# Where the first expert's weights, the prompt rows and the result tiles are moved, in a one-core mixture-of-experts step

## What is computed

```python
h2 = rms_norm(x, p['norm2_g']) * (1.0 + scale2[:, None]) + shift2[:, None]
x = x + gate2[:, None] * expert_choice_moe(h2, p['w_router'], p['w_exp_gate'], p['w_exp_up'], p['w_exp_down'])
...
    aff = jax.nn.softmax(jnp.einsum('bld,de->ble', h, w_router).astype(jnp.float32), axis=-1)
    gate, idx = lax.top_k(jnp.swapaxes(aff, 1, 2), cap)
    xs = jax.vmap(lambda hb, ib: hb[ib])(h, idx)
    hid = jax.nn.silu(jnp.einsum('becd,edf->becf', xs, w_gate)) * jnp.einsum('becd,edf->becf', xs, w_up)
    out = jnp.einsum('becf,efd->becd', hid, w_down) * gate[..., None].astype(h.dtype)
```

## Time and profile before

| what | value |
|---|---|
| median of 3 runs | 1992.8 us (1992.07 to 1993.43) |
| the profiled execution, its own time | 1993.96 us |
| its span, first to last instruction | 1992.1 us |
| mean granted TensorE clock | 0.976 |
| TensorE busy | 1906.3 us, 96% |
| VectorE busy | 1207.8 us, 61% |
| bytes read and written in DRAM | 633.46 MB and 15.38 MB |

### The profile page before, as it was taken

How to read it: one execution, slowest core, us unless ns; L and a number is a source line. 1 busy time by engine, 2 the same in 40 slices (tenths; PEclk the granted TensorE clock), 3 DMA queues, 4 the chain that set the end, 5 groups by cost and what they waited for, 6 DMA issues and landing times.

```text
span 1992.1 us, 64268 instructions
## 1 busy us (share of the span) xinstructions
PE 1906.3 (96%) x28594; PEld 1352.5 (68%) x28594; DVE 1207.8 (61%) x1966; ACT 395.3 (20%) x909; POOL 299.7 (15%) x316
## 2 busy tenths in 40 slices
PE   8999999999987999999999999999999999999996
PEld 5888899999873677777555555655556565555553
DVE  3532431232645777777677777767677676776764
ACT  4332333122320111111111111112111111111113
POOL 3032019000311010110101001010010101001002
PEclk8999999999988999999999999999999999999998
DMA  9254542322268999999999999999999999999996
GB/s 338 85 163 143 175 128 65 105 64 85 106 246 334 415 408 420 408 411 417 408 419 409 410 418 408 419 408 417 412 411 417 408 419 410 409 420 409 418 410 265
DMA packets 149503, 649.54 MB, mean 326 GB/s; under 512 B 9980, under 2 KB 54904, under 8 KB 133064
## 3 DMA queue, kind: packets, MB, share of 16 engines
q1 hardware_dynamic: 134576, 617.71, 77.0%
q0 software_dynamic: 14688, 30.98, 5.4%
q10 hardware_dynamic: 184, 0.06, 0.0%
HBM read 633.46 MB, written 15.38 MB: 326 GB/s over the span
## 4 chain that ended last, share of the span: by engine, by line
PE 43%; DMA 17%; SPq 4%; DVE 3%; issue 2%; POOL 1%; ACT 0%; DVEq 0%; POOLq 0%
PE bank L2327 17%; DMA ring<-in_w_exp_gate_dram 16%; PE bank L2355 13%; PE bank L2344 7%; PE bank L2337 5%; SPq L565 2%; SPq L572 2%; PE bank L2252 1%; DVE hid_t L1737 1%; DMA y_tile<-acc_scratch 1%; DVE sums L1672 1%; DVE hid L1741 0%; DMA x_g<-h_scratch,idx_all 0%; DVE hid_t L1744 0%; DVE hid L1734 0%
## 5 line engine op out<-in xcount | busy, mean ns | idle before, releaser
L1672 DVE TENSOR_TENSOR sums<-ring 128x704 f32<-128x704 f32 x744 | 610.4, 888 | 200.4 <-PE bank L2344 107.8
L2327 PE MATMUL bank<-ring,hid_t 128*32 128x256 f32 x8184 | 477.7, 390 | 38.7 <-DVE hid_t L1744 38.0
L2355 PE MATMUL bank<-ring,xs_t 128*32 128x352 f32 x5952 | 446.0, 459 | 0.0
L2327 PEld LDWEIGHTS bank<-ring,hid_t 128*32 128x32 f32 x8184 | 277.4, 113 | 211.9 <-DVE hid_t L1744 42.2
L2355 PEld LDWEIGHTS bank<-ring,xs_t 128*32 128x32 f32 x5952 | 198.9, 110 | 232.3 <-issue 182.3
L2344 PE MATMUL bank<-sums,xu_a 128*32 128x176 f32 x5952 | 245.1, 313 | 0.0
L2344 PEld LDWEIGHTS bank<-sums,xu_a 128*32 128x32 f32 x5952 | 194.2, 110 | 28.1
L775 POOL TENSOR_TENSOR small<-kpow 128x2 f32<-128x2 f32 x31 | 13.6, 438 | 1118.0 <-DVE out_rows L1803 882.2
L1143 ACT ACTIVATE v_both<-bank 128x176 f32<-128x176 f32 x31 | 9.8, 318 | 855.4 <-PE bank L2344 855.4
L1926 PE MATMUL bank<-act_hi,wt_hi 128*128 128x320 f32 x448 | 138.8, 310 | 0.8 <-DVE rtmp L1485 0.8
L1235 DVE TENSOR_TENSOR wt_lo<-raw_t,wt_hi 128x2048 fp32r<-128x2048 f32 x25 | 57.5, 2301 | 134.4 <-ACT wt_hi L864 134.4
(11 more groups left out here) (363 smaller groups left out, 2266.5 us busy)
## 6 DMA issues: line engine op xcount, KB each, us to landing
ring<-in_w_exp_gate_dram SPq DMA_DIRECT2D x128, 1408.0 KB, 26.1
ring<-in_w_exp_up_dram SPq DMA_DIRECT2D x128, 1408.0 KB, 27.8
ring<-in_w_exp_down_dram SPq DMA_DIRECT2D x96, 1536.0 KB, 24.9
ring<-in_w_exp_down_dram SPq DMA_DIRECT2D x32, 1024.0 KB, 27.3
raw_t<-in_w_ada_dram SPq DMA_DIRECT2D x16, 1024.0 KB, 5.2
raw_t<-in_w_in_dram SPq DMA_DIRECT2D x14, 1024.0 KB, 5.1
a_raw<-in_w_ada_dram SPq DMA_DIRECT2D x8, 1024.0 KB, 16.4
raw_t<-in_w_branch_gate_dram SPq DMA_DIRECT2D x8, 1024.0 KB, 5.4
```

The costliest lines, as they stand in the source:

```text
L1672: nc.vector.tensor_tensor(sums[:, (N_SUM * i + j) % SUM_SLOTS], w[:, k, :, n, :], w[:, kk, :, nn, :], ALU.add if sign > 0 else ALU.subtrac ...
L2327: ins = mm(bank[5 + x // 2][c * Q:(c + 1) * Q, x % 2 * DC:(x % 2 + 1) * DC], hid_t[:, f, x * Q:(x + 1) * Q], w[:, j, c * DC:(c + 1) * DC], ...
L2355: ins = mm(bank[UP_BANK[x]][c * Q:(c + 1) * Q, 0:FC], xs_t[:, x, k * Q:(k + 1) * Q], w[:, kk, c * FC:(c + 1) * FC], start=k == 0, stop=k = ...
```

## The change

- `FIRST` becomes 6. The first 8 pieces are g0, g1, u0 to u3 in slots 0 to 5, issued by SyncE, and g2, g3 in two new buffers (`extra`), issued by GpSimd once all x tiles have been written to DRAM. The buffers lie where `x2` was and `sums` will be. TensorE takes the sample groups in the order g0, g1, g2, g3, u0 to u3, and VectorE's first `sums` wait until both extra pieces are used. The rest of the stream goes into the ring from slot 6 on.
- The prompt group moves only its 16 tokens: four indirect DMAs of 16 rows in place of one of 128, in the gather and in the accumulating scatter.
- At the end the rows of the last expert are gathered first. The result tiles are loaded after the last weight piece has landed, the prompt's first. TensorE does the last piece of all three groups (prompt first) and then the three `row_sums`. ScalarE and VectorE start with the rows and take the tiles after them. The prompt rows are written after the prompt tile's store, the sample rows after the four sample stores.

The core of the diff (the helpers `y_root`, `row_square`, `row_root`, `row_sum`, `row_scale` and `y_scale` hold the instructions that stood in the loops at L1203 to L1216 and L1854 to L1875, one tile or group each):

```diff
-FIRST = 8
+FIRST = 6
+EARLY_PIECES = (("g", 0), ("g", 1), ("u", 0), ("u", 1), ("u", 2), ("u", 3), ("g", 2), ("g", 3))
+Y_ORDER = (4, 0, 1, 2, 3)
+ROW_ORDER = (2, 0, 1)
+NI = 6
...
+        extra = [at(f"extra{i}", A + 36864 + 12288 * i, [P, PIECE]) for i in range(2)]
         own_low = at("own_low", A + 59392, [P, 2, FN])
-        xu_a, xu_b = at("xu_a", 12288 + 8192, [P, KT // 2, 16, Q // 2]), at("xu_b", 98304 + 11264, [P, KT // 2, 4, Q // 2])
+        xu_a, xu_b = at("xu_a", 98304 + 8192, [P, KT // 2, 16, Q // 2]), at("xu_b", 122880 + 11264, [P, KT // 2, 4, Q // 2])
...
             for t in range(FIRST):
-                gate_up(t, t, t // 4, t % 4, 0, 0, 0)
+                gate_up(t, t, int(EARLY_PIECES[t][0] == "u"), EARLY_PIECES[t][1], 0, 0, 0)
...
-                down(STEPS * RING - 4 + i, FIRST + i, i, NE - 1, 1)
-
...
-                sp.wait_ge(s_y, lt + 1)
+                down((STEPS - 1) * RING + FIRST + i, FIRST + i, i, NE - 1, 1)
+
+            for j, lt in enumerate(Y_ORDER):
+                sp.wait_ge(s_y, j + 1)
                 dst = y_sample[0, lt * P:(lt + 1) * P, :] if lt < NS else y_prompt[0]
-                sp.dma_start(dst, y_tile[:, lt, :]).then_inc(s_out, 16)
-            sp.wait_ge(s_out, 16 * NT)
...
+            def prompt_slots(c):
+
+                return slice(c * Q, c * Q + C_P)
+
+            def gather_prompt(idx, source):
+
+                for c in range(4):
+                    pool.indirect_dma_start(x_g[prompt_slots(c), 2, :], None, source,
+                                            bass.IndirectOffsetOnAxis(idx[0:C_P, 2 + c:3 + c], 0)).then_inc(e_gath, 16)
...
-                    pool.indirect_dma_start(x_g[:, 2, :], None, h2_rows[0:4 * SPARE_END],
-                                            bass.IndirectOffsetOnAxis(idx_all[:, 0, 2:3], 0)).then_inc(e_gath, 16)
+                    gather_prompt(idx_all[:, 0, :], h2_rows[0:4 * SPARE_END])
...
             pool.wait_ge(s_acc, 16 * NT)
+            for t in range(FIRST, 8):
+                dst, landed = early_piece(t)
+                i = EARLY_PIECES[t][1]
+                pool.dma_start(dst[:, 0:2 * FH].rearrange("p (k f) -> p k f", f=FH),
+                               w_exp_gate[0, 0].rearrange("(p k) f -> p k f", k=KT)[:, 2 * i:2 * i + 2, FH:2 * FH])\
+                    .then_inc(landed, 16)
...
 
             def scatter():
-                for x in range(NX):
+                for x in range(2):
                     pool.indirect_dma_start(acc_rows, bass.IndirectOffsetOnAxis(idx_scatter[:, x:x + 1], 0), out_rows[:, x, :],
                                             None, compute_op=ALU.add).then_inc(s_acc, 16)
+                for c in range(4):
+                    pool.indirect_dma_start(acc_rows, bass.IndirectOffsetOnAxis(idx_scatter[0:C_P, 2 + c:3 + c], 0),
+                                            out_rows[prompt_slots(c), 2, :], None, compute_op=ALU.add).then_inc(s_acc, 16)
 
             pool.wait_ge(e_idx, 1)
...
-            for lt in range(NT):
-                pool.dma_start(y_tile[:, lt, :], acc_dram[scratch_rows(lt), :]).then_inc(s_fin[lt], 16)
+            pool.wait_ge(s_acc, 16 * NT + 16 * NI * (NE - 1))
...
             for x in range(NX):
                 pool.indirect_dma_start(x_g[:, x, :], None, acc_rows, bass.IndirectOffsetOnAxis(idx_all[:, NE - 1, x:x + 1], 0))\
                     .then_inc(e_gath, 16)
-            pool.wait_ge(s_out, 16 * NT)
-            for x in range(NX):
-                pool.wait_ge(s_rfin, x + 1)
+            pool.wait_ge(e_landed[FIRST + 3], 16 * STEPS)
+            for lt in Y_ORDER:
+                pool.dma_start(y_tile[:, lt, :], acc_dram[scratch_rows(lt), :]).then_inc(s_fin[lt], 16)
+            for j, x in enumerate(ROW_ORDER):
+                if j == 0:
+                    pool.wait_ge(s_outp, 16)
+                else:
+                    pool.wait_ge(s_out, 16 * NS)
...
-            act.wait_ge(e_used, RING + 3)
+            act.wait_ge(e_used, RING + 1)
             act.wait_ge(e_xt, 2)
             unit_copies(None, xs_t)
-            act.wait_ge(e_used, RING + 4)
+            act.wait_ge(e_extra, 2)
             for x in range(NX):
...
                   .then_inc(act_step, 1)
-                act.wait_ge(act_step, NT + lt + 1)
+                act.wait_ge(act_step, NT + j + 1)
                 nc.scalar.activation(small[:, 16 + lt:17 + lt], small[:, lt:lt + 1], ACT.Sqrt, bias=small[:, 46:47],
                                      scale=1.0 / D).then_inc(s_sqrt, 1)
-            for x in range(NX):
-                act.wait_ge(s_row, x + 1)
-                nc.scalar.activation(y_sq[:, x * DC:(x + 1) * DC], out_rows[:, x, :], ACT.Square,
+
+            def row_square(j):
+
+                x = ROW_ORDER[j]
+                act.wait_ge(s_row, j + 1)
+                nc.scalar.activation(hid[:, x, 0:DC], out_rows[:, x, :], ACT.Square,
                                      accum_out=small[:, 5 + x:6 + x]).then_inc(s_rsq, 1)
-                act.wait_ge(s_rsum, x + 1)
+
+            def row_root(j):
+
+                x = ROW_ORDER[j]
+                act.wait_ge(s_rsum, j + 1)
                 nc.scalar.activation(small[:, 8 + x:9 + x], bank[UP_BANK[x]][:, 0:1], ACT.Sqrt, bias=small[:, 46:47],
                                      scale=1.0 / D).then_inc(s_rroot, 1)
+
+            row_square(0)
+            row_square(1)
+            row_root(0)
+            y_root(0)
+            row_square(2)
+            row_root(1)
+            y_root(1)
+            row_root(2)
+            for j in range(2, NT):
+                y_root(j)
 
...
+            nc.vector.memset(x_g[:, 2, :], 0.0)
...
+                for c in range(1, 4) if group else ():
+                    nc.vector.tensor_scalar(idx_all[:, :, 2 + c], src[:, 0, :], 4.0, float(c), ALU.mult, ALU.add)
...
-            dve.wait_ge(e_used, RING + 3)
+            dve.wait_ge(e_used, RING + 1)
             nc.vector.memset(unit(V5)[:, :, Q // 2:], 0.0)
             nc.vector.memset(unit(V6)[:, :, 0:Q // 2], 0.0)
             unit_sums(xs_t, 1)
+            dve.wait_ge(e_extra, 2)
...
+            def y_scale(j):
+
+                lt = Y_ORDER[j]
+                dve.wait_ge(s_sqrt, 2 * NT + 1 + j + 1)
                 tick(nc.vector.reciprocal(small[:, 24 + lt:25 + lt], small[:, 16 + lt:17 + lt]))
                 nc.vector.scalar_tensor_tensor(out=y_tile[:, lt, :], in0=y_tile[:, lt, :], scalar=small[:, 24 + lt:25 + lt],
                                                in1=fg_b[:], op0=ALU.mult, op1=ALU.mult).then_inc(s_y, 1)
...
+            def row_sum(j):
+
+                x = ROW_ORDER[j]
+                dve.wait_ge(s_last, j + 1)
+                nc.vector.scalar_tensor_tensor(out=hid[:, x, 0:DC], in0=bank[x][:, 0:DC], scalar=gate_cur[:, x:x + 1],
+                                               in1=g2_q[:, x // 2, :], op0=ALU.mult, op1=ALU.mult).then_inc(e_out, 1)
+                dve.wait_ge(e_rows, NX * (NE - 1) + x + 1)
+                dve.wait_ge(e_out, done + NX + j + 1)
+                nc.vector.tensor_tensor(out_rows[:, x, :], out_rows[:, x, :], hid[:, x, 0:DC], ALU.add).then_inc(s_row, 1)
+
+            def row_scale(j):
+
+                x = ROW_ORDER[j]
+                dve.wait_ge(s_rroot, j + 1)
+                tick(nc.vector.reciprocal(small[:, 11 + x:12 + x], small[:, 8 + x:9 + x]))
+                nc.vector.scalar_tensor_tensor(out=out_rows[:, x, :], in0=out_rows[:, x, :], scalar=small[:, 11 + x:12 + x],
+                                               in1=fg_q[:], op0=ALU.mult, op1=ALU.mult).then_inc(s_rfin, 1)
+
+            dve.wait_ge(s_fg, 16 * 5)
+            dve.wait_ge(e_gath, 16 * NI * (NE - 1) + 80 + 16 * NX)
             for x in range(NX):
                 dve.wait_ge(e_out, done + x + 1)
...
+            for j in range(NX):
+                row_sum(j)
+            row_scale(0)
+            for j in range(NT):
+                y_scale(j)
+            row_scale(1)
+            row_scale(2)
...
+            def gate_up(t, tiles):
+
+                kind, i = EARLY_PIECES[t]
+                w = early_piece(t)[0][:, 0:2 * FH].rearrange("p (k f) -> p k f", f=FH)
...
-            for t in range(FIRST):
-                gate_up(t // 4, t % 4, t, (0, 1)).then_inc(e_used, 1)
+            for t in (0, 1, 6, 7, 2, 3, 4, 5):
+                gate_up(t, (0, 1)).then_inc(e_used if t < FIRST else e_extra, 1)
...
+            pe.wait_ge(e_landed[FIRST + 3], 16 * STEPS)
+            for x in ROW_ORDER:
+                down_last(x, 3).then_inc(s_last, 1)
+            for j in range(NX):
+                row_sums(j)
```

74 lines of the change are left out of this document (28 added, 46 removed).

## The result

The changed kernel took **2000.2 us** (median of 6 runs, 1997.8 to 2001.2) against 1992.8 for the kernel before (6 runs beside it, 1992.1 to 1993.8): ratio 1.0034, 95% interval 1.0024 to 1.0045. It is slower, where 1988.9 was forecast. The profiled execution took 1999.7 us, its span is 1997.8, 5.7 more than before.

A forecast was written before the change was run, and what follows sets the result against it. The weight stream with its gap was taken as the bound, TensorE following. 1993.96 - 0.7 - 6.8 + 3.6 = 1990.1 us profiled, 1.2 over the median: 1988.9; own range 1985.5 to 1992, overall range 1984.8 to 1995.2.

The forecast's parts named there:

- TensorE could do a half in 40.4 us; reserve 2.45 us a half: Expert loop: the stream needs 42.85 us a half, so TensorE keeps 56 us of reserve behind 940 us.
- Part 1, start at 628.1: Sample groups: TensorE starts at 628.1 instead of 625.21 us; two extra early weight pieces still gain 0.7 us.
- 0.9 us was allowed: Before the sample groups: added to TensorE's start because the sample gathers queue behind the extra pieces on GpSimd.
- The paragraph on the Trainium skill: Extra pieces: queues alternate one packet each; at a third of the rate, gathers are held back some 4 us more.
- Part 2, scatters -0.41 us an expert: Expert loop: the prompt scatter of 16 slots instead of 128 halves its stream cost, saving 0.41 us an expert.
- Part 2, gathers -0.16 + 0.10: Expert loop: smaller prompt gathers save 0.16 us an expert; semaphore packets of six more DMAs cost at most 0.10.
- the two slower rivals: Loop's small DMAs: few engines carry them (2014 us on 4, chance 0.06), or each has a fixed price (2048, 0.04).
- Part 3, +3.6 us: Kernel's end: tile work moved behind the rows loses its cover; last write starts at 1988.2 against 1984.58, costing 3.6 us.
- Nothing behind the last row write: Kernel's end: the forecast sum contains no term for GpSimd's closing drain.
- The worse bound of part 1: Extra early pieces: the gain was bounded at -1.5 us, with 5 us of slip in TensorE's start.
- not 4.7: Expert loop: GpSimd was to issue about 4.7 us longer, with nobody waiting.

The follow-up runs named there:

- e14: e5 plus the two extra pieces issued by GpSimd, as in the changed kernel; 1982.1 us, ratio 0.9940.
- e3: The changed kernel without the two extra pieces: eight ring pieces, old product order and buffer places; 1998.2 us, ratio 1.0018.
- e6: e5 plus the two extra pieces, issued by SyncE behind the six ring pieces instead of by GpSimd; 1980.3 us, ratio 0.9930.
- e5: The kernel before with the small scatters alone, four of 16 slots for the prompt rows; 1983.6 us, ratio 0.9947.
- e13: e5 plus the loop's four small prompt gathers alone; 1989.6 us, ratio 0.9985.
- e16: e1 plus a fourth gather of 128 slots an expert, into a place nobody reads; 1999.6 us, ratio 1.0027.
- e1: The changed kernel with the loop's prompt gather as one DMA of 128 slots again; 1992.3 us, ratio 0.9992.
- e2: The changed kernel with the prompt scatter as one DMA of 128 slots again; 2004.5 us, ratio 1.0054.
- e17: The kernel before plus 45 more indirect DMAs of 16 rows in GpSimd's idle time, outside the loop; 1995.2 us, ratio 1.0011.
- e18: e6 plus 45 more indirect DMAs in GpSimd's idle time, outside the loop; 1979.5 us, ratio 0.9929.

## Why the prediction was wrong

By its own steps:

- **"TensorE could do a half in 40.4 us; reserve 2.45 us a half".** This failed. With the small gathers TensorE needed 43.7 us for every second half. The 15 halves together took some 53 us more than 40.4 each, and the first `sums` product came 9.2 us later (656.2 against 647.0). That is 62 us, where the reserve, counted in the same way from the first `sums` products to the last (1294.4 us before, 1236 of them work), was 58. So TensorE became the bound, and its last product starts 3.8 us later than before. In e14, without pauses, part 1 costs nothing; in the changed kernel undoing it brings 3.2.
- **Part 1, start at 628.1.** It was 633.3. The four small gathers and their columns make the issue of the sample gathers 3.1 us later (2.0 predicted), but the start only 1.6 (e3). The large miss is the queue: the gathers land behind the extras, with TensorE's start 14.5 us after the issue instead of 9.6, where 0.9 us was allowed. By the starts the extras cost 6.5 us between e3 and after, and 3.9 on e5 (e14). The paragraph on the Trainium skill ("DMA: Bandwidth & Descriptors", Queues, rings and completion order) was near the size: by its turns of one packet each the pieces land near 622 and hold the gathers back 4 us more, 4.9 with the 0.9. The trace agrees: TensorE's wait for an extra ended at 623.86. I cited it and summed without it. e6 shows the cause by taking the pieces out of that queue.
- **Part 2, scatters -0.41 us an expert.** Right within 0.06: 0.35 in the stream, and e5's up passes behind 1428 us follow one another at 85.3 us (1428.5 to 1940.4, six experts), where before had 85.7.
- **Part 2, gathers -0.16 + 0.10.** Wrong in sign: +0.19 in the stream (e13). The packets of the gathers themselves do cost what was said, 47 ns for 1 KB (48 predicted). What the sum put at nothing is what they do to others: the weight packets beside them go from some 222 to 231 to 242 ns for 6 us. A row of a gather alone cannot show that. Neither of the two slower rivals was this: the price is no fixed one for each DMA, since e16 has a fourth DMA without it, and up to 7, 11 and 15 packets under way at once (gathers of 16, 32 and 64 slots) speak against 4 engines.
- **Part 3, +3.6 us.** The new end was forecast at 30.3 us and takes 29.2 in every kernel that has it. What was mis-sized is the old one: its 26.7 us held 4.7 of waiting for tiles, or 3.5 counted from the last up pass. In e5 and e6 an earlier stream frees these too. The term is 7.2 us on e5 by the medians (5.9 by the traces), so part 3 took away the larger half of what part 2 could have brought.
- **Nothing behind the last row write.** The sum has no term for GpSimd's closing drain. It gives 3.8 us to the small scatters alone and takes 3.3 with the small gathers.
- **Small ones.** The worse bound of part 1 is -1.4 by its own rows, not -1.5. GpSimd is busy 6.5 us longer an expert (396.5 against 299.7 us in 15), not 4.7; nobody waits for it.

The sum again, by one-part runs: before 0, small scatters -10.6, loop gathers +7.6, new end +7.2, first gather +0.6, part 1 -1.4: +3.4 us. Measured +6.8. The difference is within what five intervals of 2 to 3 us leave. That part 1 costs 3.2 us beside the pauses (e3) and nothing without them (e14), 4.6 us apart, is of its size; with intervals as wide it is likely and not shown.

**Open.** Why gathers into a part of the partitions slow the weight packets, and whether it is the part or the fewer rows of a DMA; why e13 has none of TensorE's pauses with the same gathers at the same stage (it differs from e3 in expert 0's gather and the end alone); and what sets the drain.

## What to carry to other kernels

A DMA is not priced by its own packets alone: look, in a trace that has both, at the packets of the stream beside it. Before moving work behind a transfer, ask whether the length of today's end is work or waiting. And here the prefetch was better in the queue of the stream that it prefetches than in the queue that the waited-for gathers use: TensorE's start came 9.8 us behind their issue and not 13.1 to 14.5. That, with the scatters, is the version worth keeping (e6, 1980.3 us).

## What had not been expected of the hardware

- While indirect gathers that fill 16, 32 or 64 partitions land, the mean 5632-byte weight packet takes 231 to 256 ns, where it takes 220 to 227 beside gathers that fill 128. Accumulating scatters of 16 rows do not do this: while an expert's scatters land it takes 223 to 225 ns with them (after, e1, e5) and 227 to 228 without (before, e2).
- TensorE can lose 3.3 us of a stage in pauses of 0.2 to 0.4 us with no releaser in the trace, while GpSimd issues such gathers, and not in every kernel that has them (e13).
- GpSimd's closing drain takes 3.7 to 9.5 us. From the last row write to the end it is 7.5 us with 6 indirect DMAs in a pass of the loop, 3.7 with 9, 4.7 and 4.9 with 10, 7.0 with 12, and 8.7 with 13; 45 more outside the loop changed nothing (e17, e18).
